# Head means of the dilated queries and keys as two rounded matmuls instead of one full-precision one

## The reference, cut to what matters

```python
proj = (h @ w_in).reshape(B, S, 3, 3, 8, 64)          # groups, (q, k, v), heads, head dim
for g, (window, dilation) in enumerate(((128, 1), (512, 4), (2048, 16))):
    q = rms_norm_2(proj[:, :, g, 0], q_gain[g]) * scale
    k = rms_norm_2(proj[:, :, g, 1], k_gain[g])       # y = x * rsqrt(mean(x*x over 64) + EPS) * gain
    o, lse = dilated_window_attention(q, k, proj[:, :, g, 2], window, dilation)
```

## Time and profile before

| what | value |
|---|---|
| median of three executions | 1596.9 us |
| the profiled execution: its time | 1600.07 us |
| its span | 1597.9 us |
| PE busy | 1549.9 us, 97% |
| DVE busy | 866.1 us, 54% |
| ACT busy | 599.4 us, 38% |
| POOL busy | 214.2 us, 13% |
| granted TensorE clock, mean | 0.993 |
| PE's share of the chain that ended last | 90% |

### The profile page before, as it was taken

How to read it: one execution, slowest core, us unless ns; L and a number is a source line. 1 busy time by engine, 2 the same in 40 slices (tenths; PEclk the granted TensorE clock), 3 DMA queues, 4 the chain that set the end, 5 groups by cost and what they waited for, 6 DMA issues and landing times.

```text
span 1597.9 us, 21136 instructions
## 1 busy us (share of the span) xinstructions
PE 1549.9 (97%) x7444; PEld 1272.8 (80%) x7444; DVE 866.1 (54%) x1135; ACT 599.4 (38%) x887; POOL 214.2 (13%) x249
## 2 busy tenths in 40 slices
PE   6999999999999999999999899999999999999998
PEld 4888777987887788888888578787997888888887
DVE  6213678436462743443332876737877767666323
ACT  6322433544234422222222622323765433334222
POOL 0010000014102400000000524333451100000000
PEclk9999999999999999999999999999999999999999
DMA  5343000431203233323323122232002233332331
GB/s 162 108 156 106 1 1 0 158 125 60 79 1 106 58 101 105 104 80 105 105 81 103 53 67 91 80 105 79 28 0 80 80 96 88 105 97 87 105 105 53
DMA packets 152796, 132.04 MB, mean 83 GB/s; under 512 B 6300, under 2 KB 137628, under 8 KB 152740
## 3 DMA queue, kind: packets, MB, share of 16 engines
q1 hardware_dynamic: 150836, 128.11, 26.0%
q0 software_dynamic: 848, 3.17, 0.6%
q10 hardware_dynamic: 1056, 0.00, 0.0%
HBM read 129.15 MB, written 2.12 MB: 82 GB/s over the span
## 4 chain that ended last, share of the span: by engine, by line
PE 90%; DVE 5%; ACT 2%; POOL 2%; issue 1%; DMA 0%; DVEq 0%; ACTq 0%; SPq 0%; POOLq 0%
PE ps L1688 25%; PE ps L1690 25%; PE ps L1689 25%; PE ps L1911 3%; PE ps L436 2%; PE ps L2021 1%; POOL x_t L741 1%; PE ps L2044 1%; DVE work L1218 1%; PE ps L469 1%; DVE a_lo L1239 1%; PE ps L1899 1%; PE ps L1928 1%; PE ps L571 1%; PE ps L2008 1%
## 5 line engine op out<-in xcount | busy, mean ns | idle before, releaser
L1688 PE MATMUL ps<-a_hi,w_hi 128*128 128x512 f32 (+2 forms) x1672 | 659.6, 394 | 16.0 <-DVE a_lo L1239 8.9
L1690 PE MATMUL ps<-a_hi,w_lo 128*128 128x512 f32 (+2 forms) x1672 | 647.1, 387 | 0.0
L1689 PE MATMUL ps<-a_lo,w_hi 128*128 128x512 f32 (+2 forms) x1672 | 646.6, 387 | 0.0
L1688 PEld LDWEIGHTS ps<-a_hi,w_hi 128*128 128x128 f32 (+1 forms) x1672 | 315.4, 189 | 91.7 <-DVE a_lo L1239 12.2
L1191 DVE TENSOR_TENSOR w_lo<-raw,w_hi 128x2048 fp32r<-128x2048 f32 x94 | 215.5, 2292 | 290.4 <-ACT w_hi L805 289.7
L1689 PEld LDWEIGHTS ps<-a_lo,w_hi 128*128 128x128 f32 (+1 forms) x1672 | 315.4, 189 | 66.3 <-issue 4.6
L1690 PEld LDWEIGHTS ps<-a_hi,w_lo 128*128 128x128 f32 (+1 forms) x1672 | 315.0, 188 | 64.5 <-issue 0.6
L805 ACT ACTIVATE w_hi<-raw 128x2048 fp32r<-128x2048 f32 x118 | 225.6, 1912 | 309.2 <-PE ps L1690 307.6
L746 POOL TENSOR_TENSOR w_lo<-raw,w_hi 128x2048 fp32r<-128x2048 f32 x24 | 110.4, 4602 | 546.2 <-ACT w_hi L805 546.2
L1551 DVE TENSOR_TENSOR arena<-ps,rstd 128x512 f32<-128x512 f32 x88 | 60.1, 689 | 173.5 <-PE ps L1690 167.2
L1621 DVE RECIPROCAL rstd<-std 128x512 f32<-128x512 f32 x24 | 80.5, 3353 | 16.8 <-ACT std L1110 16.8
(11 more groups left out here) (213 smaller groups left out, 1465.5 us busy)
## 6 DMA issues: line engine op xcount, KB each, us to landing
raw<-in_w_gate_up SPq DMA_DIRECT2D x44, 512.0 KB, 4.7
raw<-in_ffn_w_up SPq DMA_DIRECT2D x44, 512.0 KB, 4.6
raw<-in_attn_w_in SPq DMA_DIRECT2D x36, 512.0 KB, 4.2
raw<-in_w_in SPq DMA_DIRECT2D x24, 512.0 KB, 4.8
raw<-in_w_down SPq DMA_DIRECT2D x22, 512.0 KB, 4.2
raw<-in_ffn_w_down SPq DMA_DIRECT2D x22, 512.0 KB, 4.1
raw<-in_w_mem_kv SPq DMA_DIRECT2D x16, 512.0 KB, 4.1
raw<-in_w_out SPq DMA_DIRECT2D x8, 512.0 KB, 3.9
```

Source lines behind the costliest of these rows:

```text
L1688: pe.matmul(dst, s_hi, m_hi, start=start, stop=False, skip_group_check=across)
L1689: pe.matmul(dst, s_hi, m_lo, start=False, stop=False, skip_group_check=across)
L1690: return pe.matmul(dst, s_lo, m_hi, start=False, stop=stop, skip_group_check=across)
```

## The change

The squares are written twice: in full fp32 (`square`), and as a rounded upper part `square_hi` in fp32r (`square_top`), a buffer that exists once. POOL forms `square_lo`, the difference of the two, also a single buffer, in unused columns of `masks`, which grow from 896 to 1024. `mean_head` becomes fp32r (1/64 has no rounding error), and a head mean is two rounded matmuls that add up in PSUM. The head means of tiles 1 and 2 of the first group move into tiles 3 and 4. On ACT the conversion of the next chunk's weights moves from the start of a block to the end of the block before, ahead of the last root. POOL interleaves its new subtractions with those of the weights. The turns `mix`, `memo` and `dil` count on the semaphores of `mem`, which only renumbers waits.

```diff
-        mean_head = sb("mean_head", [128, 128])
+        mean_head = sb("mean_head", [128, 128], R)
+        square_hi = sb("square_hi", [128, S], R)
+        square_lo = masks[:, 512:1024]
...
             pool.memset(q_pad_2, 0.0).then_inc(pad_2_cleared, 1)
-            for c in range(1, 6):
-                split_lo(Chunk(G["dil_in"], 0, 6, c))
-            for grp in (1, 2):
-                for c in range(6):
-                    split_lo(Chunk(G["dil_in"], grp, 6, c))
+            def squares_split(n):
+                pool.wait_ge(dil_sq, n + 1)
+                pool.tensor_tensor(square_lo, squares[:, n % 2, :], square_hi[:, :].bitcast(F),
+                                   ALU.subtract).then_inc(dil_sq_lo, 1)
+            def dil_chunk(grp, c):
+                ch = Chunk(G["dil_in"], grp, 6, c)
+                if ch.first_of_gemm:
+                    squares_split(0)
+                    return
+                split_lo(ch)
+                if ch.second_of_gemm:
+                    squares_split(1)
+                if c < 4:
+                    squares_split(8 * grp + 2 * c)
+                    squares_split(8 * grp + 2 * c + 1)
+            dil_groups(pool, dil_chunk)
...
-                    act.activation(squares[:, t % 2, :], ps[:, t % 4, :], ACT.Square).then_inc(dil_sq, 1)
+                    act.activation(squares[:, t % 2, :], ps[:, t % 4, :], ACT.Square)
+                def square_top(t):
+                    n = 8 * grp + t
+                    act.wait_ge(dil_mean, n + CREDIT)
+                    act.activation(square_hi[:, :], ps[:, t % 4, :], ACT.Square).then_inc(dil_sq, 1)
...
-                if not (ch.first_of_gemm or ch.second_of_gemm):
+                if c in (0, 5) and not ch.first_of_gemm:
                     split_hi(ch)
                 if ch.first_of_gemm:
-                    square(0), square(1)
+                    square(0), square_top(0), square(1)
                     mixer_norm_out()
+                    square_top(1)
                 elif ch.second_of_gemm:
-                    square(2), root(0), square(3), root(1), root(2)
-                elif c == 0:
-                    square(0), square(1), root(0)
+                    square(2), root(0), square_top(2), square(3), root(1), square_top(3)
+                    split_hi(Chunk(G["dil_in"], grp, 6, c + 1))
+                    root(2)
                 elif c < 4:
-                    square(2 * c), root(2 * c - 1), square(2 * c + 1), root(2 * c)
+                    square(2 * c), square_top(2 * c)
+                    if c:
+                        root(2 * c - 1)
+                    square(2 * c + 1), square_top(2 * c + 1)
+                    split_hi(Chunk(G["dil_in"], grp, 6, c + 1))
+                    root(2 * c)
...
             def head_mean(n, t):
-                pe.wait_ge(dil_sq, n + 1)
+                pe.wait_ge(dil_sq_lo, n + 1)
                 if not (isinstance(n, int) and n < 2):
                     pe.wait_ge(dil_added, n - 1)
-                pe.matmul(ps[:, 4 + t % 2, :], mean_head[:, :], squares[:, t % 2, :], start=True, stop=True)\
+                pe.matmul(ps[:, 4 + t % 2, :], mean_head[:, :], square_hi[:, :], start=True, stop=False)
+                pe.matmul(ps[:, 4 + t % 2, :], mean_head[:, :], square_lo, start=False, stop=True)\
                   .then_inc(dil_mean, 1)
...
+                        if ch.second_of_gemm and j == 1 and k == 5:
+                            pe.wait_ge(norms["mixer_2"].rstd, 1)
+                            head_mean(1, 1)
+                        if grp == 0 and t == 4 and k == 3:
+                            head_mean(2, 2)
                     last.then_inc(tile_done, 1)
                     if ch.second_of_gemm and j == 0:
                         spread(norms["mixer_2"])
                         head_mean(0, 0)
-                        continue
-                    if ch.second_of_gemm:
-                        pe.wait_ge(norms["mixer_2"].rstd, 1)
-                        head_mean(1, 1)
-                    if t >= 1:
+                    elif t >= 1 and not ch.second_of_gemm:
                         head_mean(8 * grp + (t - 1), t - 1)
```

More of the change, by code:

```diff
@@ L163, in two_blocks_kernel @@
         work = sb("work", [128, 3072])
-        masks = sb("masks", [128, 896], R)
+        masks = sb("masks", [128, 1024], R)
         ident = sb("ident", [128, 128])
@@ L308, in two_blocks_kernel @@
         dil_half, dil_whole = sem("dil_half"), sem("dil_whole")
-        dil_sq, dil_mean, dil_std, dil_rstd = (
-            sem(n) for n in ("dil_sq", "dil_mean", "dil_std", "dil_rstd"))
+        dil_sq, dil_sq_lo, dil_mean, dil_std, dil_rstd = (
+            sem(n) for n in ("dil_sq", "dil_sq_lo", "dil_mean", "dil_std", "dil_rstd"))
         x_block2, x_final = sem("x_block2"), sem("x_final")
@@ L331, in __init__ @@
                 self.turned, self.hi, self.read, self.before = turned, hi, read, before
[L333 to L336, removed]
+        turns = {n: Turn(*(sem(f"{n}_{s}") for s in ("turned", "hi", "read")), 0) for n in ("x", "xs", "mem")}
+        first = turns["mem"]
+        for at, n in enumerate(("mix", "memo", "dil")):
+            turns[n] = Turn(first.turned, first.hi, first.read, (at + 1) * KT)
         VEC = {"mix_pre": 0, "mix_post": 8, "mem_pre": 16, "mem_kv_pre": 24, "mem_post": 32, "ffn_pre": 40,
@@ L1131, in half_out @@
             def half_out(f):
-                act.wait_ge(turns["dil"].turned, 2 * KT + f + 1)
+                act.wait_ge(turns["dil"].turned, 3 * KT + f + 1)
                 if f >= 2:
-                    act.wait_ge(turns["dil"].read, 2 * KT + f - 1)
+                    act.wait_ge(turns["dil"].read, 3 * KT + f - 1)
                 act.activation(dil_half_1[:, f % 2, :].rearrange("p (r b j) -> p r b j", r=4, b=4),
@@ L1392, in whole_lo @@
                 def whole_lo(f):
-                    dve.wait_ge(turns["dil"].hi, 2 * KT + f + 1)
+                    dve.wait_ge(turns["dil"].hi, 3 * KT + f + 1)
                     strided = lambda a: a[:, 4 + f, :].rearrange("p (j r) -> p r j", r=4)
@@ L1405, in _ @@
             dve.memset(eps[:, :], EPS).then_inc(const_ready, 1)
-            dve.memset(mean_head[:, :], 0.0).then_inc(pad_cleared, 1)
+            dve.memset(mean_head[:, :].bitcast(F), 0.0).then_inc(pad_cleared, 1)
             dve.wait_ge(pad_cleared, 1)
-            dve.memset(mean_head[0:64, 0:64], 1.0 / 64).then_inc(pad_cleared, 1)
-            dve.memset(mean_head[64:128, 64:128], 1.0 / 64).then_inc(pad_cleared, 1)
+            dve.memset(mean_head[0:64, 0:64].bitcast(F), 1.0 / 64).then_inc(pad_cleared, 1)
+            dve.memset(mean_head[64:128, 64:128].bitcast(F), 1.0 / 64).then_inc(pad_cleared, 1)
             dve.sem_inc(weights_split, CREDIT)
@@ L1978, in _ @@
             after = turning(turns["mix"], lambda f, b: heads_1[:, b, f * 128:(f + 1) * 128])
-            feature_major("mix_out", "", ready=turns["mix"].read, after=after, tail=1, closes=False)
+            feature_major("mix_out", "", ready=turns["mix"].read, before=KT, after=after, tail=1, closes=False)
             summed(norms["mix_post"], "mem_q")
@@ L1985, in _ @@
             after = turning(turns["memo"], lambda f, b: heads_1[:, b, f * 128:(f + 1) * 128])
-            feature_major("mem_o", "mem_q", ready=turns["memo"].read, before=KT, after=after, tail=1, closes=False)
+            feature_major("mem_o", "mem_q", ready=turns["memo"].read, before=2 * KT, after=after, tail=1, closes=False)
             summed(norms["mem_post"], "ffn_up")
@@ L2083, in _ @@
             dilated_attention()
-            feature_major("dil_out", "dil_in", tiles=4, k_tiles=4, ready=turns["dil"].read, before=2 * KT)
+            feature_major("dil_out", "dil_in", tiles=4, k_tiles=4, ready=turns["dil"].read, before=3 * KT)
             feature_major("conv_up", "dil_out", ready=norms["ffn_2"].ready, tail=1)
```

## The result

The changed kernel takes 1588.3 us (median; 1588.06 to 1588.56) where the kernel before takes 1596.9; the ratio of the two is 0.9941, with a 95% interval of 0.9928 to 0.9954. A second measurement gave 0.9952 (0.9937 to 0.9967). The forecast was 1587.3 us, faster by 0.60%; measured are 0.59% and 0.48%.

The account below looks back on a forecast made before the run. PE was taken to bound the kernel in `dil_in`. Savings of 2.65 us (first group) and 6.9 us (groups two and three) make 9.6 us, giving 1587.3 us off the 1596.9 us median; range 1584.8 to 1592.4 us.

Parts of the forecast that it names:

- The bound: In `dil_in`, PE time counts; work on ACT, POOL and DVE is free until its result comes later than PE wants.
- The head mean: On PE in `dil_in`: each head mean falls from 0.89 to 0.45 us, saving 0.433 us, 24 times, 10.4 us.
- the sum: Whole kernel: 2.65 us from the first group plus 6.9 from groups two and three, 9.6 us off.
- The chains: ACT, POOL and DVE in groups two and three meet PE's deadlines, so each group saves 3.46 us.
- the narrow place at chunk 4: Head mean of tile 7: due T + 2.74, data T + 2.6; no loss taken, 1.3 us per group at upper bounds.
- Late operands: Rival: `square_top` at 1.2 us or subtraction at 2.12 us; gain between 4 and 8 us, about 1590.5 us; chance 0.21.
- The first group: First group of `dil_in`: 2.65 us saved, against 3.46 without the losses to waits.
- the two waits: PE in the first group: some 0.8 us for tile 0's bank, 0.35 us at the head mean of tile 4.
- Edits at no cost: POOL's weights for chunk 2 start 1.3 us later; that, other conversions, `masks`, turns and memsets change nothing on PE's path.
- The rival with the other sign: POOL becomes the bound: squares' subtractions delay PE from 3.6 us each; at 4.6 us, 1611 us; chance 0.03.

Follow-up runs that it names:

- fp32_mean: Changed kernel with the head mean again one full-precision matmul over the fp32 squares, all else kept; 1598.1 us, ratio 1.000 to the kernel before.
- hi_late: Changed kernel with ACT's conversion of the next chunk's weights back at the start of its block, behind the root; 1592.5 us, ratio 0.9976 to the kernel before.
- means_late: Changed kernel with the head means of tiles 1 and 2 of the first group back behind tile 3; 1592.0 us, ratio 0.9964 to the kernel before.
- sub_2: Changed kernel with GpSimd's subtraction of squares made twice each time; 1595.1 us, ratio 0.9985 to the kernel before.
- weights_first: Changed kernel with GpSimd's first subtraction of squares behind its weights of chunk 2 instead of ahead; 1588.0 us, ratio 0.9932 to the kernel before.
- sub_3: Changed kernel with GpSimd's subtraction of squares made three times each time; 1620.6 us, ratio 1.015 to the kernel before.
- hi_twice: Changed kernel without fp32 squares and GpSimd's subtraction of squares, both head-mean matmuls reading the rounded upper squares; 1586.5 us, ratio 0.993 to the kernel before.
- after_again: Changed kernel unaltered, measured and profiled a second time against the kernel before; 1590.2 us, ratio 0.9952.
- sq_kept: Changed kernel without GpSimd's subtraction of squares, both squarings kept, both head-mean matmuls reading the upper squares; 1585.5 us in a single execution.

## Why the prediction was right

*The bound.* PE was the bound and stayed it. `fp32_mean` shows that without the cheaper head mean nothing is gained. The reordering keeps the gain: `hi_late` and `means_late` lose 2.4 us each without one of the moves.

*The head mean.* The mechanism was right and the term a little too large: 0.51 us instead of 0.45, since two steps of PE were priced like those of chunk 5. Half of the 0.06 us stays when both matmuls read the same operand, half goes; GpSimd's traffic is not the cause, as the twelve steps in `sub_2` show, and which property of `square_lo` is, stays open. In groups two and three that is 16 x 0.06 = 0.9 us: 72.4 - 69.4 = 3.0 us saved in each, not 3.46. This is nearly all of the difference between the 9.6 us of the sum and the 8.5 of the stage. The head mean before, 0.89 us, was read rightly. By the four-pass rule of the Trainium skill (FP8 and Floating Point Precision, section TensorE Precision Notes) an estimate for it is 4 x 0.2267 = 0.91 us. The trace nearly agrees; the 0.51 after is not the 0.45 of two plain steps.

*The chains.* The subtraction at 1.29 us and the second squaring at 0.59 us came in at the values taken, the root behind the conversion cost nothing in groups two and three (`hi_late`), and the narrow place at chunk 4 was passed without a wait. That it is as narrow as said `sub_2` shows: one more subtraction and PE waits 1.1 us there. Together with the waits at means 3 and 4 of the first group and DVE's longer multiplication this brings the kernel back to within 0.15% of the kernel before. "Late operands" was thus a real neighbour.

*The first group.* Sum 2.65 us, measured 8.5 - 6.0 = 2.5 us. Its parts moved: the two waits came to some 0.6 us instead of 1.15; against that 0.4 us were lost at DVE's multiplication, and eight head means cost 0.06 us more each. That these nearly cancel is luck.

*Edits at no cost.* Wrong for one of them. The subtraction ahead of the weights of chunk 2 was costed against the time when PE wants those weights; what it disturbed was DVE. GpSimd's weight subtraction now ended at 920.04, half a microsecond into an instruction of DVE with two inputs in SBUF (919.51), and that instruction ended at 920.59, 0.55 us behind GpSimd's. In `sub_2` it is the same: GpSimd ends at 924.23, DVE, begun at 922.35, at 924.78. `weights_first`, where GpSimd has ended before DVE begins, has 0.69 us. So the length goes with GpSimd's end. The Trainium skill says it (SBUF — State Buffer, section Who interferes with whom): a DVE instruction with two SBUF inputs and a GpSimd one that reads SBUF exclude each other. The prediction used the rule for GpSimd as the victim and did not look for DVE as one.

*The rival with the other sign.* Its mechanism is real (`sub_3`, slower by 1.5%), its threshold was wrong: 3.6 us was worked out with the start of the weights held fixed. The odd tile's subtraction pushes the weights, these the even tile's, and by the deadlines so corrected the limit is 2.8 us. The runs have it between 2.65 (`sub_2`, pace unchanged) and 4.0 us (`sub_3`, 14.1 us a pair).

*Profiles and medians.* The sum was made against the profiled execution and carried over to the median. That was needed: the spans of the two profiles differ by 11.7 us, the medians by 8.6, the stages by 8.5.

## What to carry to other kernels

Where PE is the bound, a single full-precision matmul of 128x512 costs nearly as much as four rounded ones (0.89 us against 0.227 us each here), and splitting its operand on idle engines pays as long as each link meets the moment at which PE wants it; write these moments down as deadlines, and let every delay push all that stands behind it in the same queue. An instruction that is moved on GpSimd has to be checked against the two-input instructions of VectorE that it now lies beside, not only against who reads its result. For an edit confined to one stage, compare that stage between the same two events, and look at the granted clock inside it. From ACT's copy on, two executions of one kernel agreed within 0.1 us, where whole executions scatter by several microseconds; up to the copy a fallen clock made 1.1 us between them.

## What the runs showed of the hardware beyond that

The scatter has a visible part. In the profile of `hi_twice` the granted clock fell to half, 1.2 GHz, behind PE's wait of 2.1 us for the reduction; the windows (columns as in the earlier trace rows):

```profile
915.00:920.00 5.00, 3.31 (x15) 2.62 (x14) 3.77 (x1) 0.55 (x2) 4.56 (x1) 0.94 0.00 0
920.00:925.00 5.00, 5.00 (x13) 3.51 (x13) 0.94 (x3) 0.26 (x1) 0.00 (x0) 0.50 0.66 210
```

From the conversion of chunk 2's weights to ACT's copy of the statistics it took 913.15 to 925.36 = 12.2 us, against 914.12 to 924.28 = 10.2 us in `weights_first`, where no such fall came. Six of the twelve profiles in the table have a fall there and six have none, although all twelve have the wait of 2.1 us; the changed kernel shows it in one execution (`after_again`) and not in the other. So the wait alone does not bring it, and what does these runs do not show. The kernel before was profiled once, without a fall; whether the change makes falls there more frequent is open. In `sub_3`, where PE waits up to 2.8 us for GpSimd again and again, the mean clock of 935 to 985 us was 0.93, in the changed kernel 1.00.

And a matmul of 128x512 is not always 0.227 us at the full clock: behind a head mean of the changed kernel twelve steps take 2.78 us, 0.232 us each, and six behind that of `sq_kept` 1.39 us.
